# Two-block fp32 forward pass on one core: a rearranged state-space stage

## The chip, the cores and the metric

One NeuronCore of a Trainium2 chip runs the whole kernel as one program. The metric is the device time of one execution in microseconds (us). TensorE (PE) multiplies, VectorE (DVE) and ScalarE (ACT) work elementwise, GpSimd (POOL) does little here, SyncE (SP) only issues DMAs. Each engine runs its own instruction list in order; semaphores order the engines among each other. A DMA is issued from SyncE's or ScalarE's list (in the profile SPq, queue q1, and ACTq, queue q10) and moved by 16 DMA engines.

## The reference

512 tokens, model width 1024, everything in fp32. Two blocks follow each other; the change lies in the first one's first layer and in the modulation vectors.

```python
# first_block, per layer l (2 layers)
shift1, scale1, gate1, shift2, scale2, gate2 = split(silu(c) @ ada_w[l] + ada_b[l], 6)
h = rms_norm(x, norm1_g[l]) * (1 + scale1) + shift1
mix = s5_mixer(h, ...)          # layer 0; layer 1 is latent attention
x = x + gate1 * mix
h = rms_norm(x, norm2_g[l]) * (1 + scale2) + shift2
x = x + gate2 * ((silu(h @ w_gate) * (h @ w_up)) @ w_down)   # F = 2816

# s5_mixer: 64 groups of 16 channels, each a 64-dim complex diagonal state
bb = f * b                      # b: (64 groups, 64 states, 16 channels), complex
s_t = a * s_{t-1} + bb u_t;  y_t = Re(c s_t) + d_skip * u_t
g = gelu(y);  return g * sigmoid(g @ w_glu + b_glu)
```

The second block (gated linear attention, a convolution branch, another SwiGLU) takes six modulation vectors of its own, from `w_ada_2`; a key/value modulation comes from `kv_ada_w`.

## The kernel before

**Weights.** Large products (`phase_pe`, L526) split activations and weights into a high and a low part and run three matmuls per 128x128 tile. ScalarE makes the high part of a weight tile (`high_part`, L506), VectorE the low one (`low_part`, L512), SyncE loads the raw tile (`load_tile`, L375) once the one before it in its buffer is split. The phases run in a fixed order: glu, then gu0, dn0, gu1, dn1 (layer 0's SwiGLU in two halves), then attention and the rest.

**Modulation.** `silu(c) @ W` is cut into chunks of 2048 columns, each made of 8 slices (128 rows x 2048 columns, 1 MB). An early slice (`early_slice`, L409) is four fp32 products of one column of silu(c) with the slice, on TensorE, into the bank AD; the profile counts 8 matmuls for it. After 8 slices ScalarE evicts the bank (`ada_evict`, L472), TensorE turns it (`ada_turn`, L478), and VectorE adds the bias (`ada_take`, L487); slice 0 of the next chunk waits for that. There are 6 early chunks: the three of `ada_w[0]` and the three of `ada_w[1]`, slices 0 to 47. Slices 0 to 7 have a buffer each, from slice 8 on four buffers are shared (`load_early`, L402): slice s is loaded once slice s-4 is used. ScalarE issues slices 0 to 3, SyncE all others. Four late chunks follow in the glu and feed-forward phases with six buffers: the first and the last with slices on TensorE, the two between as weighted sums on VectorE (`late_sum_dve`, L450 and L452), closed by four products with ones (`late_sum_pe`, L460).

**State-space stage.** `start_*` and `params_*` load x, B, C and the parameters. x is turned on TensorE (L715), and all eight parts are copied out by ScalarE (L721). B is loaded with 64-byte runs into its final order, C is turned on TensorE (L915) behind a wait for both B and C, ScalarE copies it (L777), then squares the tokens for the norm (L786) and TensorE sums them (L803). VectorE multiplies B (L761 `Bb`), makes the first inputs block and the first powers block (`inputs_dve`, `powers_dve`, L761 `WB`, `CA`, L996, L997), and then takes the first modulation chunk and writes the normalized blocks (`normed_dve`, L895). The channels go through in eight steps k of 128 (`s5_pe`, `s5_dve`, `s5_act`). In step k, TensorE turns the block (L1206, L1215), makes the states' inputs (L1229), the outputs of step k-1 (`outputs_pe`, L1259 and L1263), the kernel of step k+1 (`kernel_pe`, L1243) and turns step k-1 back (`back_pe`, L1272), with four slices between, six in step 6 and ten from step 7 on. VectorE runs the scan (`scan_dve`, L1010 to L1024), norms block k+2, and makes inputs and powers of step k+2. ScalarE copies in between: step copy L1081, inputs L1091, blocks L1099, norm bias L901, eviction of the outputs (`back_act`, L1132), kernel copy L1107 with its store to DRAM L1111; `toeplitz_act` (L1122) loads the kernel back as a Toeplitz block that `outputs_pe` of the same k reads. Four blocks of sines (`angles_act`, L954 to L959) and the rope sines (`rope_trig_act`) are in steps 0 and 1. In step 6 TensorE waits first until VectorE has made the last powers.

**Tail.** ScalarE splits two glu tiles, evicts and gelus step 7, waits until all 48 slices are done (`wait_ge(S("early_done"), 48)`), writes the eight high parts of the stage's result (L1187), and evicts the last chunk; VectorE writes the low parts (L1064). TensorE turns the last chunk, then starts the glu phase, whose first tile takes the eight parts one by one.

## Time and profile before

| | |
|---|---|
| median of 3 runs | 2411.8 us (2411.66 to 2414.57) |
| the profiled execution | 2414.91 us, span 2413.1 us |
| mean granted TensorE clock | 0.966 of full |
| TensorE busy | 2249.8 us (93%) |
| VectorE, ScalarE busy | 1090.3 us (45%), 848.8 us (35%) |
| DMA | 269.97 MB, mean 112 GB/s |

Times of rows are us from the span's start, unless marked ns. The median is a time without profiling; a row belongs to the one profiled execution.

### The profile page before, as it was taken

To read this page: it belongs to the slowest core of one execution; us is meant where nothing else is said; L and a number is where in the kernel's file an instruction comes from. 1 tells how busy PE (TensorE), PEld (TensorE's weight loads), DVE (VectorE), ACT (ScalarE), POOL (GpSimd) and SP (SyncE) were. 2 spreads that over 40 slices of the span, in tenths; PEclk is the share of its full clock that TensorE was granted. 3 is DMA by queue.
4 is the path that set the end of the run, shared out by engine and by line. 5 is a ranking of instruction groups with operands and counts; after the bars stand their busy time and mean duration, and the time that the engine had idled before them with its cause. 6 is when DMAs were issued, how large, how long until landed. Compare 5 with 4: busy or idle time off the path is not lost.

```text
span 2413.1 us, 29168 instructions
## 1 busy us (share of the span) xinstructions
PE 2249.8 (93%) x11006; PEld 1728.1 (72%) x11006; DVE 1090.3 (45%) x1583; ACT 848.8 (35%) x1310; POOL 24.5 (1%) x29
## 2 busy tenths in 40 slices
PE   4687899999998789999999999999999998999997
PEld 2443668887866556888888777676888876888885
DVE  4783345444356664534324444555424334333332
ACT  4432332222245464423223344552222223322222
POOL 2100000000000000000000000000000000000000
PEclk8798999999999799999999999999999999999998
DMA  8477545545421003233233212222333322333331
GB/s 286 169 268 283 188 136 200 187 157 186 137 80 56 6 19 97 70 107 111 72 113 106 78 53 62 60 54 54 96 96 96 96 82 67 96 107 88 97 103 58
DMA packets 360891, 269.97 MB, mean 112 GB/s; under 512 B 20402, under 2 KB 346400, under 8 KB 350544
## 3 DMA queue, kind: packets, MB, share of 16 engines
q1 hardware_dynamic: 345548, 250.00, 33.6%
q10 hardware_dynamic: 15236, 18.50, 2.5%
q8 instruction: 72, 1.18, 0.2%
q14 instruction: 35, 0.29, 0.0%
HBM read 265.39 MB, written 3.08 MB: 111 GB/s over the span
## 4 chain that ended last, share of the span: by engine, by line
PE 82%; DVE 7%; ACT 3%; DVEq 2%; DMA 2%; issue 2%; ACTq 1%; SPq 0%; POOL 0%; POOLq 0%
PE G L526 59%; PE G L2072 9%; PE MS L1402 1%; PE AD L409 1%; DVE tb L606 1%; PE MS L2301 1%; DMA ada_s<-in_ada_w 1%; PE X L2282 1%; DMA TTall<-in_s_b_im 1%; PE X L2548 1%; DVE scan L761 1%; PE X L1814 1%; DVE wlo L512 1%; DVEq L605 1%; ACT whi L506 1%
## 5 line engine op out<-in xcount | busy, mean ns | idle before, releaser
L512 DVE TENSOR_TENSOR wlo<-raw,whi 128x1024 fp32r<-128x1024 f32 (+1 forms) x296 | 380.8, 1287 | 930.3 <-ACT whi L506 927.3
L506 ACT ACTIVATE whi<-raw 128x1024 fp32r<-128x1024 f32 (+1 forms) x296 | 328.1, 1109 | 904.8 <-PE G L526 757.4
L526 PE MATMUL G<-Ahi,whi 128*128 128x512 f32 x1440 | 573.3, 398 | 16.7 <-DVE Alo L611 9.3
L526 PE MATMUL G<-Ahi,wlo 128*128 128x512 f32 x1440 | 563.8, 392 | 0.0
L526 PE MATMUL G<-Alo,whi 128*128 128x512 f32 x1440 | 563.6, 391 | 0.0
L526 PEld LDWEIGHTS G<-Ahi,whi 128*128 128x128 f32 x1440 | 272.2, 189 | 89.4 <-issue 20.2
L526 PEld LDWEIGHTS G<-Ahi,wlo 128*128 128x128 f32 x1440 | 272.4, 189 | 58.6 <-issue 3.4
L526 PEld LDWEIGHTS G<-Alo,whi 128*128 128x128 f32 x1440 | 272.2, 189 | 57.4
L526 PE MATMUL G<-mhi,whi 128*128 128x512 f32 x528 | 211.8, 401 | 0.0
L526 PE MATMUL G<-mlo,whi 128*128 128x512 f32 x528 | 205.7, 390 | 0.0
L526 PE MATMUL G<-mhi,wlo 128*128 128x512 f32 x528 | 205.4, 389 | 0.0
L2072 PE MATMUL G<-Ahi,whi 128*128 128x512 f32 x320 | 131.8, 412 | 5.3 <-DVE Alo L611 3.8
L2072 PE MATMUL G<-Ahi,wlo 128*128 128x512 f32 x320 | 125.3, 391 | 0.0
L2072 PE MATMUL G<-Alo,whi 128*128 128x512 f32 x320 | 125.2, 391 | 0.0
L526 PEld LDWEIGHTS G<-mhi,whi 128*128 128x128 f32 x528 | 99.1, 188 | 25.1 <-issue 5.3
L526 PEld LDWEIGHTS G<-mhi,wlo 128*128 128x128 f32 x528 | 99.2, 188 | 23.2 <-issue 3.1
L526 PEld LDWEIGHTS G<-mlo,whi 128*128 128x128 f32 x528 | 99.1, 188 | 21.0
L1467 ACT ACTIVATE mhi<-tb 128x512 fp32r<-128x512 f32 (+1 forms) x66 | 41.7, 632 | 148.7 <-DVEq L1494 148.7
L2072 PEld LDWEIGHTS G<-Ahi,whi 128*128 128x128 f32 x320 | 60.3, 188 | 36.9 <-issue 20.0
L1408 ACT ACTIVATE sq<-xT 128x512 f32 (+1 forms) x48 | 30.3, 632 | 118.9 <-DVEq L1511 87.6
L2072 PEld LDWEIGHTS G<-Alo,whi 128*128 128x128 f32 x320 | 60.2, 188 | 13.2
L1498 DVE TENSOR_TENSOR mlo<-tb,mhi 128x512 fp32r<-128x512 f32 (+1 forms) x66 | 45.7, 693 | 52.3 <-ACT mhi L1467 52.3
(511 smaller groups left out, 2669.0 us busy)
## 6 DMA issues: line engine op xcount, KB each, us to landing
ada_s<-in_ada_w SPq DMA_DIRECT2D x40, 1024.0 KB, 8.0
raw<-in_w_in SPq DMA_DIRECT2D x64, 512.0 KB, 4.1
ada_ff<-in_w_ada SPq DMA_DIRECT2D x24, 1024.0 KB, 6.2
raw<-in_ffn_w_gate SPq DMA_DIRECT2D x44, 512.0 KB, 3.9
raw<-in_ffn_w_up SPq DMA_DIRECT2D x44, 512.0 KB, 3.9
raw<-in_ffn_w_down SPq DMA_DIRECT2D x32, 704.0 KB, 4.7
raw<-in_w_ffn_in SPq DMA_DIRECT2D x44, 512.0 KB, 3.8
raw<-in_w_ffn_out SPq DMA_DIRECT2D x16, 704.0 KB, 4.7
```

Source lines behind the costliest of these rows:

```text
L409: mm = E.eng.matmul(AD[32 * b:32 * b + n, :], cv, buf[:, b * 512:(b + 1) * 512], start=k == 0, stop=k == KD - 1)
L506: last = E.eng.activation(whi[j][:, k0:k0 + k, 0:c], raw[j][:, k0:k0 + k, 0:c], ACT.Copy)
L512: last = E.eng.tensor_tensor(wlo[j][:, k0:k0 + k, 0:c], raw[j][:, k0:k0 + k, 0:c], whi[j][:, k0:k0 + k, 0:c].bitcast(FP32), ALU.subtract)
L526: mm = E.eng.matmul(out_, a[j][:, k0 + kk, 0:c], b(kk), start=first and kk == 0 and n == 0, stop=last and kk == k - 1 and n == 2)
L605: E.eng.drain()
L606: E.eng.scalar_tensor_tensor(tb[k % 2][:, 0:n], src(k), a(k), rstd[:, 0:n], ALU.mult, ALU.mult)\
L761: E.eng.tensor_tensor(o, a, b, op)
L1402: E.eng.matmul(MS[:, :], ones, sq[j][:, :], start=first, stop=last).then_inc(S("sq_free"), 1)
L1408: E.eng.activation(sq[j][:, :], xT[:, bass.ds(n, 1), :].rearrange("p o t -> p (o t)"), ACT.Square)\
L1467: E.eng.activation(mhi[:, bass.ds(u, 1), :].rearrange("p o t -> p (o t)"), tb[1][:, :], ACT.Copy)\
L1498: E.eng.tensor_tensor(mlo[:, bass.ds(u, 1), :].rearrange("p o t -> p (o t)"), tb[1][:, :], mhi[:, bass.ds(u, 1), :].rearrange("p o t -> p ...
L2072: mm = E.eng.matmul(out_, a[j][:, kk, :], b[:, kk, :], start=first and n == 0, stop=last and n == 2)
```

## The change

1. **Chunks.** Chunk 2 of `ada_w[1]` (scale2 and gate2 of layer 1) leaves the early slices (40 instead of 48) and becomes a third VectorE sum among the late chunks (40 late loads instead of 32): dn0 now takes two sums per pair of tiles, gu1 one in eight pairs, and the last chunk's slices move from gu1 to dn1. In the loop each step has four slices.
2. **Start.** B is loaded as 32 rows of 8 KB and turned by 32 transposes into two PSUM banks, from which VectorE multiplies. The C transposes wait for C alone. ScalarE issues slices 0 to 7 and copies four x parts, VectorE the other four. ScalarE copies C after the token squares. All TensorE transposes of C and B come before slice 0; the norm sum before slice 2. VectorE makes the first powers after the two first normalized blocks.
3. **ScalarE in the loop.** In each step the output eviction and the kernel copy come before the norm bias; sines are spread over steps 0 to 2, rope sines and the gelu table go from step 1 to step 2; the Toeplitz load is issued after the blocks of its own step in each step, for step 7 too.
4. **Tail.** The last early chunk is evicted and turned before, high and low parts 0 to 6 are written before the eviction of step 7, part 7 after it.

```diff
+        Brow = [t[0:NPAIR, :, :].rearrange("p a b -> p (a b)")[:, 0:P * NCH] for t in (Wall, CAall)]
+        Braw = [X[1 + i].rearrange("p (c r) -> p r c", c=NCH) for i in range(2)]
...
+        ADA = ((A["ada_w"][0], 0, 1), (A["ada_w"][0], 1, 1), (A["ada_w"][0], 2, 1), (A["ada_w"][1], 0, 1),
+               (A["ada_w"][1], 1, 1), (A["kv_ada_w"], 0, 1), (A["w_ada_2"][0], 1, 1), (A["w_ada_2"][0], 2, 1),
+               (A["ada_w"][1], 2, 1), (A["w_ada_2"][0], 0, 2))
+        NEARLY_C = 5
+        NEARLY_S = NEARLY_C * KD
+        NADA = 5 * KD
...
-                d(Braw[i], A[f"s5_b_{w}"][0].rearrange("(r a) n p -> (a n) r p", a=2)).then_inc(S("dma_bc"), 16)
-            for s in range(4, 8):
-                load_early(E, s)
+                d(Brow[i], A[f"s5_b_{w}"][0].rearrange("(r a) n p -> r (a n p)", a=2)).then_inc(S("dma_b"), 16)
...
-            for n in range(4):
+            for n in range(KD):
                 load_early(E, n)
-            x_copy_act(E, 0, 4)
+            x_copy(E, 0, 4)
...
-            x_copy_act(E, 4, KD)
-            E.eng.wait_ge(S("ct_done"), E.nth("ct_done"))
+        def c_rows_act(E):
+
+            E.eng.wait_ge(S("turned_in"), 2)
...
+            c_rows_act(E)
             a.wait_ge(S("sq_free"), E.ahead("sq_free", 2))
             a.wait_ge(S("sd_free"), E.nth("sd_free"))
             a.activation(rstd[:, :], MS[:, :], ACT.Copy).then_inc(S("ms_done"), 1)
+            E.eng.wait_ge(S("xt_done"), KD)
...
+            x_copy(E, 4, KD)
...
             inputs_dve(E, 0)
-            E.eng.wait_ge(S("c_taken"), 1)
-            powers_dve(E, 0)
             ada_take(E, 0)
             gain_scale(E, acol[:, :], V_N1, mod[0][:, 8:16], 0)
             rms_dve(E)
             normed_dve(E, 0)
             normed_dve(E, 1)
+            E.eng.wait_ge(S("c_taken"), 1)
+            powers_dve(E, 0)
             inputs_dve(E, 1)
             powers_dve(E, 1)
...
+            E.eng.wait_ge(S("dma_c"), E.nth("dma_c", 2))
             E.eng.wait_ge(S("vec_ready"), 1)
             for i in range(2):
                 for t in range(8):
                     mm = E.eng.transpose(CBANK[2 * i + t // 4][0:NST, (t % 4) * P:(t % 4 + 1) * P], Craw[i][:, t, :],
                                          ident)
-            mm.then_inc(S("ct_done"), 1)
-            for s in range(2, 4):
+            mm.then_inc(S("turned_in"), 1)
+            E.eng.wait_ge(S("dma_b"), E.nth("dma_b", 2))
+            E.eng.wait_ge(S("xt_copied_2"), 4)
+            for i in range(2):
+                rows = Brow[i].rearrange("r (m c) -> r c m", c=NCH)
+                for c in range(NCH):
+                    mm = E.eng.transpose(X[1 + i][:, c * NPAIR:(c + 1) * NPAIR], rows[:, c, :], ident[0:NPAIR, 0:NPAIR])
+            mm.then_inc(S("turned_in"), 1)
+            E.eng.wait_ge(S("silu_c"), 1)
+            for s in range(2):
                 early_slice(E, s)
             token_rms_pe(E)
-            for s in range(4, 8):
+            for s in range(2, KD):
                 early_slice(E, s)
             ada_turn(E, 0)
             E.eng.wait_ge(S("c_taken"), 1)
             turn_inputs_pe(E, 0)
             E.eng.wait_ge(S("ms_done"), E.ahead("ms_done", 1))
-            kernel_pe(E, 0)
...
+            def low(k):
                 E.eng.wait_ge(S("hi_ready"), E.nth("hi_ready"))
                 v.tensor_tensor(Alo[:, k, :], hS[:, k, :], Ahi[:, k, :].bitcast(FP32), ALU.subtract)\
                     .then_inc(S("part_ready"), 1)
+
+            for k in range(KD - 1):
+                low(k)
+            out_dve(E, 7)
+            v.drain().then_inc(S("s5_out"), 1)
+            low(KD - 1)
             v.drain().then_inc(S("in_ready"), 1)
-            ada_take(E, 5)
+            ada_take(E, 4)
...
                     blocks_act(E, 0)
-                    toeplitz_act(E, 0)
+                    kernel_act(E, 0)
                 else:
                     steps_act(E, k)
                 if k < 7:
                     turn_steps_act(E, k + 1)
                     inputs_act(E, k + 1)
-                else:
-                    ada_evict(E, 4)
                 if k > 0:
                     blocks_act(E, k)
-                    if k < 7:
-                        toeplitz_act(E, k)
-                if k < 6:
-                    normed_act(E, k + 2)
+                toeplitz_act(E, k)
                 if k == 6:
                     kernel_act(E, 7)
                 if k > 0:
                     back_act(E, k - 1)
                 if k < 6:
                     kernel_act(E, k + 1)
-                if k > 1:
+                if k < 3:
+                    angles_act(E, k + 1)
+                if k == 2:
+                    rope_trig_act(E)
+                    preset(E, ACT.Gelu_apprx_tanh)
+                if k < 6:
+                    normed_act(E, k + 2)
+                if k == 3:
+                    gelu_act(E, 0)
+                if k > 2:
                     gelu_act(E, k - 2)
                 if k in (1, 3, 5):
                     ada_evict(E, k // 2 + 1)
-                if k == 0:
-                    angles_act(E, 1)
-                if k == 1:
-                    angles_act(E, 2)
-                    angles_act(E, 3)
-                    rope_trig_act(E)
-                    preset(E, ACT.Gelu_apprx_tanh)
-                if k == 6:
-                    toeplitz_act(E, 7)
             high_part(E, "glu", 0, 0)
             high_part(E, "glu", 1, 1)
             gelu_act(E, 6)
+            E.eng.wait_ge(S("early_done"), NEARLY_S)
+            ada_evict(E, 4)
+            a.drain()
+
+            def high(k):
+                a.activation(Ahi[:, k, :], hS[:, k, :], ACT.Copy).then_inc(S("hi_ready"), 1)
+
+            for k in range(KD - 1):
+                high(k)
             back_act(E, 7)
             gelu_act(E, 7)
             a.drain()
-            E.eng.wait_ge(S("early_done"), 48)
-            for k in range(KD):
-                a.activation(Ahi[:, k, :], hS[:, k, :], ACT.Copy).then_inc(S("hi_ready"), 1)
-            ada_evict(E, 5)
+            high(KD - 1)
...
+                    kernel_pe(E, 0)
...
+                slices(s, 11 + 4 * k)
+                if k < 6:
+                    kernel_pe(E, k + 1)
+                if k > 0:
+                    back_pe(E, k - 1)
+                slices(11 + 4 * k, 12 + 4 * k)
             outputs_pe(E, 7)
-            slices(42, 45)
+            ada_turn(E, 4)
             back_pe(E, 7)
-            slices(45, 48)
-            ada_turn(E, 5)
...
+            first, n = {"gu0": (6, 1), "dn0": (17, 2), "gu1": (25, 1), "dn1": (36, 1)}.get(ph, (None, 0))
             if first is None:
                 return None
-            return {i: lambda s=first + i: load_late(E, s) for i in range(TILES[ph] // 2)}
+
+            def loads(i):
+                for s in range(first + n * i, first + n * i + n):
+                    load_late(E, s)
+            return {i: lambda i=i: loads(i) for i in range(TILES[ph] // 2)}
...
+                return {0: lambda: late_sum_pe(E, 6), 1: lambda: ada_turn(E, 6)}
             if ph == "gu1":
-                return {6: lambda: late_sum_pe(E, 8), 7: lambda: ada_turn(E, 8),
-                        8: lambda: late_slice(E, 24), 9: lambda: late_slice(E, 25)}
+                return {0: lambda: late_sum_pe(E, 7), 1: lambda: ada_turn(E, 7),
+                        8: lambda: late_sum_pe(E, 8), 9: lambda: ada_turn(E, 8)}
+            if ph == "dn1":
+                return {0: lambda: late_slice(E, 32), 1: lambda: late_slice(E, 33)}
...
+                sums = {"gu0": {i: (5 + i,) for i in range(3, 11)},
+                        "dn0": {i: (16 + 2 * i, 17 + 2 * i) for i in range(4)},
+                        "gu1": {i: (24 + i,) for i in range(8)}}[ph]
+                takes = {"gu0": {3: 5}, "dn0": {1: 6}, "gu1": {1: 7, 9: 8}}[ph]
```

## Rows read from the trace of the kernel before

**Rows 1.** The page's part 4: chain that ended last, share by engine.

```profile
PE 82%; DVE 7%; ACT 3%; DVEq 2%; DMA 2%; issue 2%; ACTq 1%; SPq 0%; POOL 0%; POOLq 0%
```

**Rows 2.** Windows: length, PE PEld DVE ACT POOL busy, clock, DMA share, GB/s.

```profile
202.00:246.00 44.00, 30.94 (x292) 11.66 (x281) 11.02 (x23) 9.29 (x15) 0.00 (x0) 0.84 1.01 352
...
320.00:600.00 280.00, 279.81 (x1250) 227.55 (x1250) 127.73 (x114) 77.38 (x93) 0.00 (x0) 1.00 0.54 180
```

**Rows 3.** Timeline of the start: start, us, line, operation, [idle before, releaser].

```profile
12.61 15.93 SPq L663 DMA_DIRECT2D TTall<-in_s_b_im  x1
...
33.49 1.84 PE L915 MATMUL X<-con,TTall 128*64 128x128 f32 x8 [2.35 <-DMA TTall<-in_s_b_im]
...
41.62 1.06 ACT L786 ACTIVATE CA<-turned 128x1024 f32<-128x1024 f32 x1
...
50.84 3.49 PE L409 MATMUL AD<-ada_first,cact 128*1 128x512 f32 x16
...
54.16 1.89 PE L409 MATMUL AD<-hS,cact 128*1 128x512 f32 x16
...
58.19 1.78 DVE L895 SCALAR_TENSOR_TENSOR tb<-xT,acol,rstd 128x512 f32<-128x512 f32 x1 [0.26 <-issue]
```

**Rows 4.** DMA: queues in 18 to 20 us; one issue with us to landing.

```profile
q10 hardware_dynamic: 112, 0.79, 95.9%
q1 hardware_dynamic: 112, 0.03, 6.7%
...
TTall<-in_s_c_im SPq DMA_DIRECT2D x1, 256.0 KB, 21.7
```

**Rows 5.** Timeline: eight transposes of 64 rows at half clock.

```profile
110.98 1.12 PE L1215 MATMUL X<-con,Hn 64*128 64x64 f32 x8 [5.13 <-ACTq L1083]
```

**Rows 6.** Windows around the C transposes (columns as in rows 2).

```profile
34.00:36.00 2.00, 2.00 (x12) 1.59 (x11) 1.97 (x4) 0.00 (x0) 0.00 (x0) 0.50 0.98 410
...
38.00:40.00 2.00, 0.87 (x11) 0.00 (x0) 1.93 (x5) 1.94 (x6) 0.00 (x0) 1.00 0.98 414
```

**Rows 7.** Timeline: the last operation of the first powers block.

```profile
44.95 0.75 DVE L997 SCALAR_TENSOR_TENSOR CA<-CA,c 128x576 f32<-128x576 f32 x1
```

**Rows 8.** Timeline of steps 1 to 3, ScalarE and VectorE.

```profile
105.18 0.63 ACT L954 ACTIVATE turned<-ang 128x512 f32<-128x512 f32 x1
...
109.85 1.05 ACT L1081 ACTIVATE Hn<-X 64x512 f32<-64x512 f32 x2
...
116.01 1.42 DVE L761 TENSOR_TENSOR scan<-X,turned 128x256 f32<-128x256 f32 x4 [9.55 <-PE X L1229]
...
129.62 1.07 ACT L1081 ACTIVATE Hn<-X 64x512 f32<-64x512 f32 x2 [0.23 <-PE X L1206]
...
135.00 1.42 DVE L761 TENSOR_TENSOR scan<-X,turned 128x256 f32<-128x256 f32 x4 [1.84 <-PE X L1229]
```

**Rows 9.** Timeline of step 6's end, step 7 and the tail.

```profile
204.16 0.71 PE L1272 MATMUL X<-con,Ypk 64*128 64x64 f32 x8
...
211.95 1.89 PE L409 MATMUL AD<-ada_s,cact 128*1 128x512 f32 x8 [7.09 <-DMA ada_s<-in_ada_w]
...
216.05 1.92 PE L1206 MATMUL X<-con,tb 128*64 128x128 f32 x8
...
232.45 0.44 PE L1263 MATMUL G<-TTall,Ust 128*64 128x128 f32 x4
...
234.95 1.20 ACT L1132 ACTIVATE Ypk<-G 64x512 f32<-64x512 f32 x2
...
245.24 4.27 ACT L1187 ACTIVATE Ahi<-hS 128x512 fp32r<-128x512 f32 x8 [6.30 <-PE AD L409]
...
250.95 0.77 PE L526 MATMUL G<-Ahi,whi 128*128 128x512 f32 x1
```

**Rows 10.** Late sums by tile, ns min/median/max; window of a dn0 pair.

```profile
L452 DVE SCALAR_TENSOR_TENSOR ada_sum<-ada_ff,cact,ada_sum x14: 2341/2346/2348, 378.4 to 559.7; 128x2048 f32<-128x2048 f32 x14
...
469.00:484.00 15.00, 15.00 (x70) 12.41 (x69) 5.94 (x6) 2.76 (x2) 0.00 (x0) 1.00 0.66 228
```

More of the change, by code:

```diff
@@ L160, in program @@
         c2 = sb("c2", [P, 4, RB + 1, NCH], where=s5a)
-        Wst = [[sb(f"Wst{k}{i}", [P, 4, P], where=s5a) for i in range(2)] for k in range(2)]
+        Wall = sb("Wall", [P, 4, 4 * P], where=s5a)
+        Wst = [[Wall[:, 2 * k + i, :].rearrange("p (a b) -> p a b", a=4) for i in range(2)] for k in range(2)]
         ada_first = [sb(f"ada_first{i}", [P, 2 * D], where=s5a) for i in range(2)]
@@ L209, in program @@
         xn = turned[:, :, :]
-        CA = [[sb(f"CA{k}{i}", [P, 4, RB + 1, NCH], where=s5) for i in range(2)] for k in range(2)]
+        CAall = sb("CAall", [P, 4, 4 * (RB + 1) * NCH], where=s5)
+        CA = [[CAall[:, 2 * k + i, :].rearrange("p (a b c) -> p a b c", a=4, c=NCH) for i in range(2)] for k in range(2)]
         CA2 = sb("CA2", [P, 2, 4 * (RB + 1) * NCH], where=s5)
@@ L1184, in s5_act @@
             a.drain()
-            E.eng.wait_ge(S("early_done"), 48)
-            for k in range(KD):
-                a.activation(Ahi[:, k, :], hS[:, k, :], ACT.Copy).then_inc(S("hi_ready"), 1)
-            ada_evict(E, 5)
+            high(KD - 1)
         def turn_inputs_pe(E, k):
@@ L1332, in early_sp @@
                 load_tile(E, "glu", n, n)
-            for s in range(44, 48):
-                load_early(E, s)
         def phase_sp(E, ph, hooks=None):
@@ L1581, in ffn_hooks_act @@
         def ffn_hooks_act(E, ph):
-            if ph in ("gu0", "dn0", "gu1"):
-                i, c = {"gu0": (2, 6), "dn0": (0, 7), "gu1": (6, 8)}[ph]
-                return {i: lambda: ada_evict(E, c)}
+            rows = {"gu0": {2: 5}, "dn0": {0: 6}, "gu1": {0: 7, 8: 8}, "dn1": {}}.get(ph)
+            if rows is not None:
+                return {i: lambda c=c: ada_evict(E, c) for i, c in rows.items()} or {99: None}
             if ph == "gu2":
@@ L3047, in _ @@
             turn_steps_act(E, 0)
-            kernel_act(E, 0)
             normed_act(E, 1)
```

120 lines of the change are left out of this document (47 added, 73 removed).

## The prediction, made before the changed kernel was run

> **What bounds the kernel now.** I read the chain that ended last first: TensorE holds 82% of it, almost all in the 3-pass weight products at L526 [rows 1]. The stage table then says where TensorE is not the bound. From 320 to 600 us it is busy 279.81 of 280.00 us, so there a microsecond of VectorE or DMA work is free and one of TensorE is not. From 202 to 246 us it is busy 30.94 of 44.00 us at a clock of 0.84 while the DMA engines stand at a share of 1.01 [rows 2]. The change edits the first 251 us, so I went on with the timeline of that stretch: the start, the eight steps of the state-space loop, the tail. Every term below is a wait of that timeline that goes, moves or appears.
>
> **Start, up to the first normalized block (58.19 us).** SyncE's issue of the second B load alone takes 15.93 us; TensorE (for the C transposes behind the same semaphore) and VectorE wait for its landing until 33.49. ScalarE waits for the turned C, copies it, and only then starts the token squares at 41.62. Modulation slices 4 to 7 are queued behind the norm on TensorE and start at 50.84, though slices need nothing of it; the last ends at 56.05 [rows 3].
>
> After the change the squares start when ScalarE has finished the trigonometry (it has nothing to wait for there), VectorE takes four of its x copies, and C is copied after the squares. TensorE becomes the long chain: C transposes, B transposes, slices 0 and 1, the norm sum, slices 2 to 7. When does C land? Its second half is issued after some 6 us of small loads and lands 21.7 us later, near 28. In 18 to 20 us both queues moved exactly 112 packets each, though 0.79 MB against 0.03 MB [rows 4]: one packet of C's 256 bytes for one of 8 KB of the modulation weights. The Trainium skill, DMA: Bandwidth & Descriptors, Queues, rings and completion order, states such a round robin by packets, and the trace agrees. So twice as many modulation slices on ScalarE's queue can only delay C, and B stands behind C. B however is now 64 packets of 8 KB instead of 8192 of 64 bytes: 4 to an engine. I take C at 28.5 and B at 31.5. C's first eight transposes took 1.84 us at half clock [rows 3], 16 take 3.6: done at 32. B's 32 transposes have no row; the nearest are eight of 64x64 in 1.12 us at half clock [rows 5] (0.14 each, 4.5 us) and C's (0.23 each, 7 us); I take the small ones, as B's have 32 columns: done at 36.5. Two slices cost 1.89 us at full clock and 3.49 at half [rows 3]. Eight at full: 7.6. The norm sum, eight small products, I estimate at the 1.84 of C's eight: 2. Then eviction, turn and take as before (56.05 to 58.19): 2.1. Sum 48.2; I take 49, bounds 46 (C not delayed, small transposes) and 55.
>
> The other bound is the clock. The Trainium skill, TensorE: Matmul & The Clock Gate, Part 4: PE-mode transpose, says that transposes do not raise the clock; by it all eight slices would run at half clock, 14 us instead of 7.6, and the block would come at 55. The trace says otherwise: granted clock 0.50 in 34 to 36 us, where TensorE ran only transposes, and 1.00 in 38 to 40 us [rows 6]. I keep the full clock.
>
> Against it stands the order on VectorE. The first powers block (six operations of 0.75 us, started some 0.7 apart: 4.3 us) used to fill the wait for the slices (it was done at 45.70) [rows 7] and now lies between the first normalized block and the first scan. VectorE was already back to back there, so it costs its full 4.3. **Start: 9.2 - 4.3 = +4.9 us** (bounds -1 and +8).
>
> **Loop, steps 0 to 5.** Step 0 is VectorE's own work, unchanged. In step 1 ScalarE no longer stands at the norm wait before it evicts, and one of two angle blocks, the rope sines and the Gelu table go to step 2. VectorE waited 9.55 us for scan 2; without it the powers of step 3 are just finished when the states come: **+9.5**. What left step 1 is from 105.18 to 109.85, 4.7 us, plus the shift of 0.7; in step 2 they now stand between the kernel copy and the step copy at 129.62, where ScalarE had only 0.23 us idle. That copy begins the chain that VectorE waits 1.84 us for at 135.00, so all of it shows: **-4.6** [rows 8]. In steps 3 and 5 VectorE alone is the bound (before scan 4 and after scan 5 it has no wait in the trace), and in step 4 the slices wait for the modulation taken after the scan, as before: **0**.
>
> **Step 6.** Six slices before the next turn, with four buffers: after the back-turn at 204.16 TensorE waits 7.09 us for slice 36 and turns the next block at 216.05. With a chunk fewer only slice 35 is left there, already moved in exchange from before the back-turn. From 204.87 to 216.05 are 11.2 us. Slice 36 now stands before the states of step 7, some 6 us after the back-turn, at 211; it landed at 211.95, its load starting as early after as before: **+11**, bounds +8 and +11.
>
> **Step 7 and tail.** Outputs of step 7 end at 232.89. Then came: eviction at 234.95, the wait for slice 47 until 245.24 (6.30 us on ScalarE), eight high parts in 4.27 us, the last modulation turn, first product at 250.95: 18.1 us after the outputs [rows 9]. After: two weight splits, gelu 0.6, eviction 0.6, seven high parts 3.7 (all startable before the outputs end), then eviction 1.2, back-turn 0.7 and the first product, because parts 0 to 6 are ready; 21 products cover the last part's 3 us. The weight tiles land some 3 us before the outputs end, so about 4 us of the high parts stick out: first product 6.3 us after the outputs. The last Toeplitz load is issued in step 7 instead of step 6 and has 9 us before its use; it moves 0.5 MB beside four slices. I allow 2 us for it and slices 37 to 39. **+10**, bounds +6 and +12.
>
> **Later.** The chunk comes back as eight VectorE sums in dn0 and gu1 at 2.35 us, hidden: a dn pair has VectorE busy 5.94 of 15.00 us with one sum in it. The eight more loads are hidden too: that pair moved 228 GB/s at a share of 0.66 [rows 10]. On TensorE, which is the bound there, four ones-products (as long as one slice) and four turns are new: 0.95 + 0.7 = **-1.7**. The same eight two-row slices move from gu1 to dn1.
>
> Sum: 4.9 + 9.5 - 4.6 + 11 + 10 - 1.7 = 29.1 us of the profiled execution's 2414.91. That one lies 3.1 us above the median 2411.8; I take the difference off the median: 2382.7, so **2383 us**.
>
> **Rivals.**
> *The start gives nothing.* If eight large loads starve C and B, or the transposes are slow, the first block comes at 55 and the 4.3 us of powers eat the rest: gain 23, 2389 us. For: the one-to-one packets. Against: C needed only until 28.1 with the same arbitration. 0.14.
> *Step 2 is absorbed.* If the sines find a gap in ScalarE's 9 us wait before the scan, the -4.6 goes: 2378; with the start at its best, 2375. Against: program order puts them after the kernel copy. 0.12.
> *The last loads stick.* Slice 36 holds the states of step 7, or the Toeplitz block comes 4 us late behind 8 KB packets: gain 22, 2390 us. For: slice 36 landed 7.09 us after TensorE stood ready for it, with the DMA engines full [rows 2, 9]. 0.14.
> *Nothing moves.* If the 44 us were bound by TensorE after all; its 30.94 busy us speak against. 2412, 0.02.
> *Slower.* One place: the dn0 and gu1 pairs. Their VectorE orders two sums of 2.35 us (dn0), one (gu1), ahead of the next low split. If the split comes after the tile before it ends, TensorE waits in each of 12 pairs. The place turns the result only when each wait exceeds 29/12 = 2.4 us, a whole sum: 2.35 on 8 more sums is 19 us, 2402 us; with waits of 3 us 2419 us. Against: 5.94 + 2.35 of 15.00. 0.04.
>
> **Chances.** The sum as worked out 0.54. About 0.2% (5 us) is what a measurement of this kernel can tell from none. Faster 0.94, same 0.02, slower 0.04. The range goes from the best start with step 2 absorbed (2373) to two of the losing rivals together (2397).
>
> **What the profile of after would show.** First normalized block near 49 us and scan 0 about 5 us earlier; VectorE without a wait before scan 2; the step copy of step 3 later after the kernel copy than 0.9 us, with sines between; no wait over 3 us for a slice at the end of step 6; first product near 220 us; sums of 128x2048 at 24, not 16, and TensorE still busy throughout 320 to 600. Wrong would be: C landing past 32 us; TensorE waiting for the Toeplitz load; TensorE waits for low splits in dn0.

## The result, and the profile after

The changed kernel takes 2390.74 us (median of 4 runs, 2387.76 to 2391.8), the kernel before 2411.97 (4 runs): ratio 0.991, 95% interval 0.9894 to 0.9926, so 21.2 us less. I had said 2383, 29.1 less. The profiled execution took 2387.76 against 2414.91, which is 27.2 less; it is 3 us under its median, and the profiled execution of before is 3 us above its own, so some 6 us of that difference are not the change's.

The chain of waits is as before [rows 1]: the weight products keep it. The first line is the page's share by engine, the others are windows (columns as in rows 2). The stage from 320 to 600 us is still TensorE's, and the one after the last scan now stands at 208 to 216:

```profile
PE 82%; DVE 7%; ACT 3%; DVEq 3%; DMA 2%; issue 2%; ACTq 1%; SPq 0%; POOL 0%; POOLq 0%
...
320.00:600.00 280.00, 280.00 (x1255) 227.97 (x1255) 145.11 (x122) 77.42 (x92) 0.00 (x0) 1.00 0.58 198
...
188.00:192.00 4.00, 4.00 (x40) 2.70 (x38) 3.72 (x10) 0.59 (x1) 0.00 (x0) 0.54 0.34 95
192.00:196.00 4.00, 4.00 (x49) 2.15 (x53) 1.69 (x6) 0.73 (x2) 0.00 (x0) 1.00 0.10 21
...
204.00:208.00 4.00, 4.00 (x64) 2.73 (x59) 3.32 (x8) 0.00 (x0) 0.00 (x0) 1.00 1.00 408
208.00:212.00 4.00, 3.00 (x32) 1.00 (x34) 3.08 (x8) 1.82 (x3) 0.00 (x0) 1.00 1.09 185
212.00:216.00 4.00, 1.27 (x14) 0.54 (x8) 0.00 (x0) 0.00 (x0) 0.00 (x0) 0.95 0.96 171
```

DMA is nearly idle at 188 to 196 (shares 0.34 and 0.10) and full at 208 to 216, there at 171 to 185 GB/s where almost nothing but slices ran at 408 just before. This contrast decides the tail, below.

The start, as a timeline (start, us, line, operation, idle before). It answers to rows 3 and 7:

```profile
28.73 1.91 PE L928 MATMUL X<-con,TTall 128*64 128x128 f32 x8 [5.32 <-DMA TTall<-in_s_c_im]
...
32.85 1.98 PE L936 MATMUL X<-con,Wall 32*128 32x32 f32 x16 [0.51 <-DMA CAall<-in_s_b_im]
34.65 1.95 PE L936 MATMUL X<-con,CAall 32*128 32x32 f32 x16
36.53 3.59 PE L417 MATMUL AD<-ada_s,cact 128*1 128x512 f32 x16
40.05 1.84 PE L818 MATMUL MS<-sq,con 128*128 128x128 f32 x8
...
49.28 2.51 DVE L911 SCALAR_TENSOR_TENSOR tb<-xT,acol,rstd 128x512 f32<-128x512 f32 x2 [0.26 <-issue]
```

The reader sees the chain that I had added up: C at 28.5 (28.73), B's transposes done at 36.5 (36.6), the normalized block at 49 (49.28). Steps 1 and 2 answer to rows 8:

```profile
103.91 1.42 DVE L773 TENSOR_TENSOR scan<-X,turned 128x256 f32<-128x256 f32 x4 [1.87 <-PE X L1253]
...
114.93 0.59 ACT L1130 ACTIVATE KT<-MS 48x512 f32<-48x512 f32 x1 [4.87 <-PE MS L1267]
...
116.39 0.63 ACT L974 ACTIVATE turned<-ang 128x512 f32<-128x512 f32 x1 [0.87 <-ACT KT L1130]
...
121.67 1.05 ACT L1104 ACTIVATE Hn<-X 64x512 f32<-64x512 f32 x2
...
127.45 1.42 DVE L773 TENSOR_TENSOR scan<-X,turned 128x256 f32<-128x256 f32 x4 [6.38 <-PE X L1253]
```

The sines stand between the kernel copy and the step copy, as foreseen, and VectorE waits 6.38 us for scan 3; but there is a hole of 4.87 us ahead of the kernel copy. The tail answers to rows 9:

```profile
203.19 0.60 ACTq L1145 DMA_DIRECT2D TTall<-blocks  x1
...
204.49 1.42 DVE L773 TENSOR_TENSOR scan<-X,turned 128x256 f32<-128x256 f32 x4 [4.79 <-PE X L1253]
...
211.72 1.04 PE L417 MATMUL AD<-ada_s,cact 128*1 128x512 f32 x8 [1.00 <-DMA ada_s<-in_ada_w]
...
215.49 1.07 PE L1283 MATMUL G<-CAall,Sst 64*64 64x128 f32 x8 [2.73 <-DMA TTall<-blocks]
...
218.22 1.06 ACT L515 ACTIVATE whi<-raw 128x1024 fp32r<-128x1024 f32 x1 [0.56 <-DMA raw<-in_s_w_glu]
...
220.50 3.75 ACT L1205 ACTIVATE Ahi<-hS 128x512 fp32r<-128x512 f32 x7
...
224.15 1.18 ACT L1155 ACTIVATE Ypk<-G 64x512 f32<-64x512 f32 x2
...
226.18 0.79 PE L535 MATMUL G<-Ahi,whi 128*128 128x512 f32 x1
```

Two transfers are late here: the last Toeplitz block holds the output products until 215.49, and the second glu weight tile lands at 218.22, 17.7 us after its issue, with seven copies and the last Y copy queued behind it on ScalarE.

One edit that "The change" does not name bears on this. The kernel before issued the first two glu weight tiles ahead of its last four slices (44 to 47); the changed kernel issues them behind its last slice. SyncE's lists, first before, then after (the x4 of the last line takes in the next two tiles, issued from 219 us on):

```profile
220.67 4.73 SPq L375 DMA_DIRECT2D raw<-in_s_w_glu  x2
227.63 7.48 SPq L402 DMA_DIRECT2D ada_s<-in_ada_w  x4
```

```profile
196.24 3.65 SPq L410 DMA_DIRECT2D ada_s<-in_ada_w  x4
199.93 21.00 SPq L378 DMA_DIRECT2D raw<-in_s_w_glu  x4
```

**Scan by scan.** Each step is the time from one scan's start to the next (first operation of the scan on VectorE). "Tail" goes from the last scan to the first glu product, "rest" from there to the end of the span. Step k goes from scan k to scan k+1. All are profiled executions; the last three columns are experiments below.

| | before | after | chunk alone (e9) | e6 | e8 |
|---|---|---|---|---|---|
| scan 0 at | 69.55 | 64.91 | 68.23 | 69.09 | 64.40 |
| step 0 | 20.52 | 20.75 | 20.51 | 20.99 | 20.36 |
| step 1 | 25.94 | 18.25 | 25.92 | 18.12 | 16.32 |
| step 2 | 18.99 | 23.54 | 18.98 | 23.58 | 19.63 |
| steps 3 to 5 | 59.24 | 60.14 | 60.33 | 59.53 | 59.91 |
| step 6 | 28.58 | 16.90 | 18.22 | 15.72 | 15.73 |
| tail | 28.13 | 21.69 | 24.36 | 14.40 | 14.40 |
| rest | 2162.2 | 2159.7 | 2159.2 | 2158.7 | 2158.0 |

### The profile page after: what moved, and what is told of

The parts are those of the page before. It is cut to its first block, busy times and chain, and to the rows that moved or that the text cites. A ratio compares the mean times of both kernels' runs of the same rounds, so it can differ in the third digit from the quotient of the medians.

```text
span 2385.9 us, 29083 instructions
## 1 busy us (share of the span) xinstructions
PE 2240.0 (94%) x10982; PEld 1728.6 (72%) x10982; DVE 1110.4 (47%) x1595; ACT 846.0 (35%) x1306; POOL 24.4 (1%) x29
## 3 DMA queue, kind: packets, MB, share of 16 engines
q1 hardware_dynamic: 336844, 245.80, 33.5%
## 4 chain that ended last, share of the span: by engine, by line
PE 82%; DVE 7%; ACT 3%; DVEq 3%; DMA 2%; issue 2%; ACTq 1%; SPq 0%; POOL 0%; POOLq 0%
PE G L535 60%; PE G L2089 9%; PE MS L1412 1%; DVE tb L615 1%; PE AD L417 1%; PE MS L2318 1%; PE X L2299 1%; DMA CAall<-in_s_b_im 1%; DMA raw<-in_s_w_glu 1%; PE X L2565 1%; PE X L1831 1%; DVE wlo L521 1%; DVEq L614 1%; ACT whi L515 1%; DVEq L774 1%
## 5 line engine op out<-in xcount | busy, mean ns | idle before, releaser
L1418 ACT ACTIVATE sq<-xT 128x512 f32<-128x512 f32 (+1 forms) x48 | 30.3, 632 | 117.7 <-DVEq L1521 86.6
L2089 PEld LDWEIGHTS G<-Alo,whi 128*128 128x128 f32 x320 | 60.5, 189 | 13.2
```

What stands on the lines that cost most here:

```text
L1418: E.eng.activation(sq[j][:, :], xT[:, bass.ds(n, 1), :].rearrange("p o t -> p (o t)"), ACT.Square)\
L2089: mm = E.eng.matmul(out_, a[j][:, kk, :], b[:, kk, :], start=first and n == 0, stop=last and n == 2)
```

## The experiments

Medians are compared with the changed kernel's 2390.74 and, for the parts made alone, with the runs of the kernel before that were measured beside them. A "ratio" or "of before" is always against those runs of before, with its 95% interval.

### e1 to e3: is the tail held by the Toeplitz block or by the weight tiles?

e1 issues the last Toeplitz load at the end of step 6:

```
-                toeplitz_act(E, k)
+                if k < 7:
+                    toeplitz_act(E, k)
...
+                if k == 6:
+                    toeplitz_act(E, 7)
```

> The changed kernel with one edit: the load of the last Toeplitz block is issued at the end of step 6 again, as before the change, not in step 7. In the changed kernel it is issued at 203.2 us and holds up the last output products until 215.5, and the first glu product comes at 226.2. Theory A (the two glu weight tiles, which land at 216.6 and 218.2, and the split, the eviction and the seven copies that ScalarE runs behind them, set the first product): the block lands by 211, the last output products start near 212.8, but ScalarE still comes to the last Y copy near 224, the first product stays within 1 us of 226.2 and the time within 1.5 us of 2390.7. Theory B (the late Toeplitz block sets it): the first product comes 3 to 4 us earlier, 2387.

e2 places the weight splits behind the copies and the last Y copy (low_part likewise behind out_dve):

```
-            high_part(E, "glu", 0, 0)
-            high_part(E, "glu", 1, 1)
             gelu_act(E, 6)
...
             back_act(E, 7)
+            high_part(E, "glu", 0, 0)
+            high_part(E, "glu", 1, 1)
             gelu_act(E, 7)
```

> The changed kernel with one edit: on ScalarE and VectorE the seven copies and differences of A, the last Y copy and the last output sum are placed ahead of the splits of the first two glu weight tiles. The last Toeplitz block still lands at 215.5. Theory A (the weight tiles gate the first product by ScalarE's order): the copies run near 213.5 to 217.3, the last Y copy at 221 (end of the output products), the split behind it, and the first product comes near 223.2, 3 us earlier; 2387.7. Theory B (the Toeplitz block and what follows its products alone set it): the Y copy was not held, the first product stays near 226, 2390.7, or later by the 2.1 us of the splits that now stand behind the Y copy, 2393.

e3 has both edits.

> Both edits together, on the changed kernel: the Toeplitz load back at the end of step 6, and the weight splits behind the copies and the last Y copy. Theory A with the Toeplitz block as the second gate behind it: output products from 212.8 to 216.5, Y copy at 217.3, first product at 219.5 to 220.5, 6 to 6.5 us earlier; 2384.5. If one of the two alone were the gate, this kernel would give no more than that one alone (3 to 4 us). If the DMA engines are simply full until 218, so that the blocks only change places, the weight tiles land later than 218.2 and the gain is below 3.

Measured: 2393.66 (e1), 2392.83 (e2), 2394.11 us (e3); tails 22.65, 21.35 and 22.04 us. None of them gained anything. In e1 the output products no longer wait for the Toeplitz block, but the last but one and the last slice came later:

```profile
215.15 1.88 PE L417 MATMUL AD<-ada_s,cact 128*1 128x512 f32 x8 [3.01 <-DMA ada_s<-in_ada_w]
...
218.01 1.89 PE L417 MATMUL AD<-ada_s,cact 128*1 128x512 f32 x8
219.83 1.12 PE L1286 MATMUL G<-CAall,Sst 64*64 64x128 f32 x8
```

Its last scan began at 206.53, so the outputs start 13.3 us behind it, against 11.0 in the changed kernel. In e2 the copies of A were done by 220.8, but the Y copy waited for the output products until 225.31 and the splits came behind it. So the Toeplitz block alone is not the gate: the time is the one that theory A of e1 gives, but the block's early load delayed slices, and the outputs did not start at 212.8. ScalarE's order alone is not the gate either (theory B in e2), and neither are the two together. What holds is the last sentence of e3's expectation: the DMA engines are full, and blocks only change places.

### e6: give the tail's DMA work an idle time

```
-            for s in range(KD, NEARLY_S):
+            for s in range(KD, 36):
                 load_early(E, s)
             for n in range(2):
                 load_tile(E, "glu", n, n)
+            for s in range(36, NEARLY_S):
+                load_early(E, s)
```

> The changed kernel with one edit: SyncE issues the loads of the first two glu weight tiles ahead of slice 36, not behind slice 39. Between 180 and 196 us the DMA engines are nearly idle (0.16 and 0.36 of their time), while slices 36 to 39 wait for their buffers; from 200 to 216 they are full. Theory A (what the tail lacks is DMA time between 200 and 218: swapping ScalarE's order or issuing the Toeplitz block earlier only moved the wait, the first product came 21.7, 22.7, 21.4 and 22.0 us after the last scan began): the tiles land before 195, the last slice and the Toeplitz block within 13 us after the last scan began... worked from the changed kernel: slice 39 and the block by 210 to 211, the last output products 211.7 to 215.4, seven copies 213 to 217, Y copy 217, first product near 219.5 instead of 226.2, counted from the last scan 15 us instead of 21.7; total 6 to 7 us less than the changed kernel. Theory B (ScalarE's and TensorE's own chain behind the last scan is 21 us long whatever lands when): no change within 1 us.

Measured 2382.94 us (4 runs, ratio to before 0.9886, interval 0.9868 to 0.9905), 7.8 less than the changed kernel. The tiles are now issued at 177.19, ahead of the last four slices, which is the place that they had in the kernel before. The tail is 14.40 us, 7.3 less (e8, with the same edit, has 14.40 too), and windows of the same stretch read:

```profile
184.00:188.00 4.00, 4.00 (x20) 3.51 (x18) 0.06 (x1) 2.20 (x3) 0.00 (x0) 0.50 0.86 216
...
212.00:216.00 4.00, 2.83 (x32) 1.12 (x24) 3.64 (x6) 3.80 (x7) 0.00 (x0) 1.00 0.26 73
```

Timeline of the same kernel, whose last scan began at 207.03:

```profile
177.19 3.79 SPq L378 DMA_DIRECT2D raw<-in_s_w_glu  x2
...
215.48 0.65 PE L1283 MATMUL G<-CAall,Sst 64*64 64x128 f32 x8 [1.13 <-DMA TTall<-blocks]
...
221.43 0.50 PE L535 MATMUL G<-Ahi,whi 128*128 128x512 f32 x1
```

Theory A is shown by size and place, to within 1 us of what was expected: the two tiles, loaded in the full stretch, were the price, and the change had put them there itself.

### e4 and e10: the start

e4 builds the first powers block ahead of the take again:

```
             inputs_dve(E, 0)
+            E.eng.wait_ge(S("c_taken"), 1)
+            powers_dve(E, 0)
             ada_take(E, 0)
...
-            E.eng.wait_ge(S("c_taken"), 1)
-            powers_dve(E, 0)
```

> The changed kernel with one edit: VectorE builds the first block of powers again ahead of the take of the first modulation row. VectorE is idle there from 44.5 to 48.5 us, and the block of powers takes 4.3 us (51.7 to 56.0) behind the normalized blocks. Theory A (my term of the start: the move costs what it adds ahead of the first scan): the first normalized block stays at 49.3 to 49.8, the first scan comes at 60.9 instead of 64.9, and all later scans with it: 4 us, 2386.7. Theory B (the first two steps are set by ScalarE and TensorE, so that a first scan that is earlier is given back by the third): the scan of step 2 moves by under 1 us and the time stays at 2390.7 within 1 us.

Measured 2398.05 us (2397.48 to 2400.94), 7.3 more. Scan 0 came at 64.61 with C landed at 31.08, but step 1 grew from 18.25 to 23.33. The first states and the first kernel product came later (63.99, against 59.90), so did the first Toeplitz load (71.44, against 66.66), and TensorE met it missing:

```profile
71.44 0.70 ACTq L1145 DMA_DIRECT2D TTall<-blocks  x1
...
87.23 1.12 PE L1283 MATMUL G<-CAall,Sst 64*64 64x128 f32 x8 [2.86 <-DMA TTall<-blocks]
```

Both theories missed, the first with the wrong sign. The move that I priced at -4.3 us is worth more than it costs. Counted from C's landing, this kernel's scan 0 is some 2 us earlier (33.5 us behind it, against 35.4 on average in the seven profiles listed below), its first glu product 2.1 us later (199.5 us behind it, against 197.4 in the changed kernel). Of the remaining 5 us I know only that they lie behind the first product (rest 2165.4 in the one profile).

e10 is the kernel before with the changed start alone (the diff of the start functions, and kernel_act and kernel_pe of block 0 moved into step 0).

> The kernel before with the start of the change alone (B as rows turned on TensorE, half of the turned x copied by VectorE, all eight first slices issued by ScalarE, normalized blocks ahead of the powers of block 0, first kernel product behind the first states). Theory A (what the runs so far say): the first scan comes at 65 to 69 instead of 69.6, with C's landing as the cause of the spread; 1 to 2 us less than before, 2410.5. Theory B (my term of the start, 4.9 us): 2407. If the new place of the first kernel product delays the first Toeplitz block where ScalarE's order is the old one, step 0 or 1 is longer and the time is 2412 or more.

Measured 2413.78 us (11 runs, 2406.86 to 2424.21) against 2411.96 (17 runs, 2408.99 to 2415.39): ratio 1.0001, interval 0.9989 to 1.0014. The start alone gives nothing that can be measured, at most 2.7 us, and widens the spread from 6 to 17 us. In its one profile C landed at 32.80 and scan 0 began at 68.30, 1.25 us earlier than in the first profile of before; steps 0 to 4 are as before, but steps 5 and 6 and the tail are longer by 0.73, 1.55 and 0.45 us, so that its first glu product is 1.4 us later (252.36). With 48 early slices TensorE waits for slices there (2.48 and 5.91 us at the end of step 6), whatever the start gained. So e10 prices the start in the old loop, not in the changed one.

### e12 and e5: why the start gives so little

> The kernel before once more, for its profile alone: is its start as variable as that of the changed one, and how long is what follows the first glu product? If C's landing varies here too, the first scan is not at 69.6 but anywhere in 67 to 73. If only the changed start varies, it is at 69.6 within 0.5. From the first product to the end of the span the changed kernel and its variants took 2158 to 2165 us with the same code, the kernel before 2162.2; it should fall into this band.

2410.55 us. TensorE's first C transposes, in this order: in e12 ([rows 3] has the other profile of before), in e9, which has the old start, and in e3, the latest of the profiles with the changed start:

```profile
33.52 1.92 PE L915 MATMUL X<-con,TTall 128*64 128x128 f32 x8 [2.80 <-DMA TTall<-in_s_b_im]
```

```profile
33.55 1.16 PE L921 MATMUL X<-con,TTall 128*64 128x128 f32 x8 [1.95 <-DMA TTall<-in_s_b_im]
```

```profile
34.53 1.91 PE L928 MATMUL X<-con,TTall 128*64 128x128 f32 x8 [11.11 <-DMA TTall<-in_s_c_im]
```

With the old start C and B had both landed by 33.49, 33.52 and 33.55. With the changed one, C alone had landed at 28.73, 31.31, 31.97, 33.09, 33.19, 33.29 and 34.53 (after, e11, e1, e2, e7, e6, e3), and scan 0 began at 64.91, 66.43, 67.42, 68.34, 68.60, 69.09 and 69.33: mean 67.7. Before it began at 69.55, 68.78 and 68.23 (e9): mean 68.9. The start gives 1.1 us on average, and my profile of the changed kernel is its luckiest start. (Two more profiles have the same start loads: C at 31.08 in e4 and at 32.80 in e10.)

The landing of C by itself says why. Here are the loads of its second half, with us from issue to landing, in the second profile of before, in the changed kernel and in e3:

```profile
TTall<-in_s_c_im SPq DMA_DIRECT2D x1, 256.0 KB, 21.8
...
TTall<-in_s_c_im SPq DMA_DIRECT2D x1, 256.0 KB, 22.3
...
TTall<-in_s_c_im SPq DMA_DIRECT2D x1, 256.0 KB, 28.1
```

With the old start it took 21.7 ([rows 4]), 21.8 and 21.4 us, with the changed one 22.3 to 28.1. The changed start no longer makes C wait for B, which had come last, and at the same time it made C land later, by up to 6.7 us.

e5 gives slices 4 to 7 back to SyncE, behind B:

```
-            for n in range(KD):
+            for n in range(4):
                 load_early(E, n)
...
+            for s in range(4, KD):
+                load_early(E, s)
```

> The changed kernel with one edit: the first slices 4 to 7 (4 MB) are issued by SyncE behind the loads of B, as before the change, not by ScalarE ahead of them. In four kernels with the changed start the imaginary part of C landed at 28.7, 32.0, 33.1 and 34.5 us, and the first scan followed 36.2, 35.5, 35.3 and 34.8 us behind it (64.9 to 69.3). Theory A (the eight slices on ScalarE's queue share the DMA engines with C's and B's small runs and set when they land, and how much by chance): C lands by 27 and with less spread, the slices 4 to 7 land last, near 42 to 44, so that the last of their products end near 46 and the first scan comes at 62 to 65; 2387 to 2389. Theory B (C's descriptors are what is slow, whoever shares the engines): C lands at 28 to 35 as before, the first scan at 65 to 69, and the time is that of the changed kernel, 2390.7 to 2393, or more if the slices are late.

2387.4 us (5 runs, 0.9897 of before, interval 0.988 to 0.9913); C at 30.39, scan 0 at 65.14; in e8, which has the same edit, 29.57 and 64.40. Two landings, both earlier than six of the seven above, and 3.3 us off the median: it leans to theory A, but the intervals overlap with the changed kernel's and C never landed by 27. Likely, not shown. And it would not be the whole: with four slices on ScalarE's queue, as before the change, C still took 24.0 and 23.2 us, 1.4 to 2.6 more than with the old start. The other difference beside it is B's form, rows of 8 KB in place of 64-byte runs on C's own queue; no run changes that alone.

### e7 and e11: step 1 and step 2

e7 moves the sines into ScalarE's hole ahead of the kernel copy, in steps 0 to 2:

```
-                if k < 6:
-                    kernel_act(E, k + 1)
                 if k < 3:
                     angles_act(E, k + 1)
                 if k == 2:
                     rope_trig_act(E)
                     preset(E, ACT.Gelu_apprx_tanh)
+                if k < 6:
+                    kernel_act(E, k + 1)
```

> The changed kernel with one edit: in steps 0 to 2 ScalarE computes the angles' sines (in step 2 also the rotary sines and the switch to the Gelu table) ahead of the kernel copy, where in step 2 it is idle for 4.9 us (from 110.1 to 114.9), and not behind it. Theory A (my term of step 2: the 4.6 us that step 2 lost are this block of 4.6 us ahead of the normalized block and the step copy): step 2, from scan 2 to scan 3, falls from 23.5 us to 19 to 20; step 1 may gain up to 1; total 4 us less than the changed kernel. Theory B (the step copy of step 3 waits for something else, so the block is hidden): step 2 stays at 23.5 within 1 us and the time with it.

2388.16 us (4 runs, 2387.62 to 2389.07), 2.6 less. Step 1 is 16.32 us, step 2 20.63, together 4.8 less; step 4 took 1.65 more. Theory A, with a little less in step 2 and more in step 1. A timeline line of step 2 shows the kernel copy of this kernel with the sines done before it and still 2.67 us idle:

```profile
118.23 0.59 ACT L1130 ACTIVATE KT<-MS 48x512 f32<-48x512 f32 x1 [2.67 <-PE MS L1267]
```

e11 undoes "evictions ahead of the norm wait": normed_act stands again directly behind toeplitz_act.

> The changed kernel with one part undone: ScalarE's normalized block of each step stands again behind the Toeplitz load and ahead of the copies of Y and of the kernel, so that these wait for VectorE's normalized block. Theory A (my term of step 1, measured as 8.0 us, is this order): step 1 rises from 18.3 us to 24 to 26, steps 2 to 5 by up to 1 each; 8 to 10 us more than the changed kernel, 2400. Theory B (step 1's gain came from the sines of angles 3, the rotary sines and the table switch, 4.6 us that moved from step 1 to step 2): step 1 rises by 3 or less, 2394.

2389.99 us (6 runs; 0.9914 of before, interval 0.99 to 0.9929), the time of the changed kernel; step 1 is 19.02 us, 0.8 more, which is no more than the spread: e3 and e5, without this edit, have 18.98 and 19.01. ScalarE waits 11.64 us for VectorE's normalized block again, and it doesn't matter:

```profile
93.88 0.72 ACT L917 ACTIVATE hS<-tb,mod 128x512 f32<-128x512 f32 x1 [11.64 <-DVE tb L911]
...
100.08 0.60 ACT L481 ACTIVATE arow<-AD 128x512 f32<-128x512 f32 x1
100.58 1.06 ACT L1104 ACTIVATE Hn<-X 64x512 f32<-64x512 f32 x2
```

From the normalized block to the step copy ScalarE needed 12.81 us before (97.04 to 109.85) and needs 6.70 here: the 4.7 us of sines and table are gone, and the eviction at L481, ahead of which ScalarE stood idle for 2.32 us before, now has the other sines in front of it. Here is the kernel before at that place:

```profile
97.04 0.72 ACT L901 ACTIVATE hS<-tb,mod 128x512 f32<-128x512 f32 x1 [11.69 <-DVE tb L895]
...
101.92 0.60 ACT L472 ACTIVATE arow<-AD 128x512 f32<-128x512 f32 x1 [2.32 <-PE AD L409]
```

### e9: the chunk alone

The kernel before with 40 early slices, the new late tables and hooks, and the old start and orders.

> The kernel before with one part of the change alone: the sixth modulation chunk is computed in the later phases (40 early slices, not 48; the late tables and hooks as in the changed kernel); start, ScalarE's order in the steps and the order of the tail stay as before. Theory A (the terms of step 6 and of the tail are the chunk's): scans 0 to 6 as before (69.6 to 194.2, within the start's spread), step 6 falls from 28.6 to 17 us, step 7 and tail from 28.1 to 22 to 24, later phases 2 us later; 15 to 16 us less than before, 2396. Theory B (the new orders carry the tail, so that without them the products of A and the weight tiles give it back): 9 to 11 us less, 2402.

2398.72 us (5 runs, 2395.91 to 2400.57), ratio 0.9945, interval 0.9932 to 0.9957: 13.2 less than before, between the theories. It has the glu tiles behind the last slice, as the changed kernel has. Step 6 gives 10.4 and the tail 3.8 (table). With the rest of the change the tail is 2.7 shorter still (24.36 to 21.69): here ScalarE's eight copies still stand behind the last Y copy, and TensorE's last wait is for the modulation eviction behind them:

```profile
235.78 1.12 PE L484 MATMUL AD<-con,arow 128*128 128x128 f32 x4 [6.46 <-ACT arow L478]
```

### e8: the three edits that helped

e5, e6 and e7 together, on the changed kernel.

> The changed kernel with the edits of the three kernels before: slices 4 to 7 behind B, glu tiles ahead of slice 36, sines ahead of the kernel copy. Theory A of each, added: start 2 to 4, step 2 4, tail 6 to 7: 12 to 15 us less than the changed kernel, 2377 to 2380. If they are not independent (a step that starts earlier waits longer for slices or for the Toeplitz blocks), 6 to 9 us less, 2383.

2371.87 us (5 runs, 2370.49 to 2375.34; 0.9835 of before, interval 0.9821 to 0.9849): 40.3 us less than the kernel before, 18.9 less than the changed one, above the 12 to 15 I expected and above the sum of the three medians (3.3 + 7.8 + 2.6 = 13.7). First glu product at 210.75, 15.4 us ahead of the changed kernel's profile; its start is early too (64.40), which is some 3 us against the mean start of 67.7, and makes 18 or so. This version beats both kernels.

## Why the prediction held, and where it was off

The time lay in my range and on the side that I gave 0.94, 7.7 us above my value. The signs and places of the terms are right but for the powers; the start and the tail each fell some 4 us short and step 1 another 2; the total stayed in the range (2373 to 2397) because the range was wide enough for both. Two of the three signs that I had named as "wrong would be" came true: C landed past 32 us in most profiles with the changed start (not in the changed kernel's own), and TensorE waited 2.73 us for the last Toeplitz load. Two of my rivals came true by about half, "the start gives nothing" (priced at -6 us, measured -3.8) and "the last loads stick" (-7, measured -3.6 in the tail, by the Toeplitz block and not by slice 36). The terms, against the table; the start is taken from the means over profiles, because single profiles mislead there:

| term | predicted | measured |
|---|---|---|
| start | +4.9 | +1.1 (e10, in the old loop: 0, up to 2.7) |
| step 0 | 0 | -0.2 |
| step 1 | +9.5 | +7.7 |
| step 2 | -4.6 | -4.6 |
| steps 3 to 5 | 0 | -0.9 |
| step 6 | +11 | +11.7 |
| step 7 and tail | +10 | +6.4 |
| later | -1.7 | not seen: rest 2158.6 to 2162.2 before, 2158.0 to 2165.4 with it |
| sum | 29.1 | 21.2 (medians: 21.2) |

That the sum meets the medians this closely is partly chance: only the start is a mean, the other rows are one pair of profiles, and the rest of the span is not in it. Other profiles with the same code in a row give step 1 from 18.1 to 19.0, step 6 from 15.7 to 16.9 and the tail from 21.6 to 22.1 us.

**Start.** The failed step is "I take C at 28.5". When C came at 28.73 the links behind it came as added up (B at 32.8 for 31.5, but TensorE was busy with C until 32.3; B's transposes done at 36.6 for 36.5; the block at 49.28 for 49). But C came there once in seven. I had written that eight slices on ScalarE's queue can only delay C and that C past 32 us would prove me wrong; it landed past 32 in four of seven (five of nine with e4 and e10). My first rival, "the start gives nothing", had the block at 55; in the seven profiles it came at 49.28 to 53.65. Its mechanism, that large loads starve C, fits the landings, but only leans on e5. Between 18 and 20 us the two queues again moved packets nearly one for one, ScalarE's 8 KB ones against C's 256 bytes:

```profile
q10 hardware_dynamic: 112, 0.79, 96.0%
q1 hardware_dynamic: 113, 0.03, 6.7%
```

The -4.3 of the powers failed in sign (e4): on VectorE's own list it does cost its time, but the first normalized block is also the head of the chain to the first Toeplitz block, which step 1 needs.

The clock term was off as well. I kept the full clock for all eight slices, but in every profile with the changed start the first two took 3.20 to 3.59 us, at or near half clock; the other six went at 1.90 a pair. That is up to 1.7 us of the chain. In the changed kernel the granted clock stayed at 0.50 through all transposes (28.73 to 36.6) and up to 40 us. In e2 it did rise while TensorE ran nothing but transposes (33.09 to 40.77), and fell again to 0.56 in 40 to 42; the line is a window, columns as in rows 2:

```profile
38.00:40.00 2.00, 2.00 (x21) 2.00 (x20) 0.00 (x0) 1.79 (x5) 0.00 (x0) 1.00 1.02 406
```

So both happen with this code, and my row of 38 to 40 us could not promise either.

**Step 1.** The size was nearly right, the first of its two reasons wrong. I named that ScalarE no longer stands at the norm wait and that sines and table leave the step. e11 puts the wait back, and it costs 0.8 us at most. What carried the step, by e11's rows, is that 4.7 us of sines and table left it and that the 2.3 us idle ahead of the modulation eviction was filled; no run puts the sines back, so this is read, not tested. The missing 1.8 us are the angle block that stayed: with it ahead of the kernel copy step 1 is 16.32 us (e7), VectorE's own work without a wait, 9.6 less than before.

**Step 2.** Right in place and size. But "all of it shows" was a matter of position only: the hole ahead of the kernel copy takes most of it (e7). The rival "absorbed" was one swap away.

**Step 6.** Right: slice 36 no longer stands there. Of the 11.7, 10.4 come with the chunk alone (e9).

**Tail.** The failed step is "I allow 2 us for it and slices 37 to 39". What follows the output products shrank from 18.1 us to 5.3 (I had 6.3). But the outputs themselves end 16.4 us after the last scan instead of 10.1: 6.3 us, not 2, for one Toeplitz block, two weight tiles and the slices, all issued between 196 and 204 us. I looked at the block's size and its nine us, not at the sum of what was on the DMA engines in that time, and not at the glu tiles, which the change moved behind the last slice; with them back ahead of the last four slices the tail is 14.40 us (e6), 13.7 less than before, where I had forecast 10. "The weight tiles land some 3 us before the outputs end" was true (218.22 and 220.84), but only because both were late.

**Later.** The sums are 24 (21 and 3 of the first kind), TensorE is busy 280.00 of 280.00 us from 320 to 600, so they are hidden. Whether the 1.7 us on TensorE are there can't be told: the rest of the same code varies by 7 us between profiles. The mean granted clock of the whole execution varies too (0.967 to 0.977), but it does not order them: e11 had 0.977 and a rest of 2160.4 us, e5 0.971 and 2158.1.

## What to carry to other kernels

When a wait for a transfer goes, look at the DMA row of the windows around it before moving issues within it: if it is full there and empty ahead, try a load with free buffers in the empty stretch (7.8 us here); swapping the loads or the order of their readers gave nothing in three kernels. When loads are taken off a queue's list, look where that leaves the others on it: here two tiles slid behind the last slice unpriced. A profile is one draw: scan the same stage in several profiles before a term is booked to it; here the start's 4.6 us of the first pair of profiles were 1.1 on average. And a block taken off one engine's list is not free or dear by itself: ask which chain its neighbour heads (e4), and whether the engine has a hole one place further up (e7).

## What the runs showed of the hardware

- How long a 256 KB load of 256-byte runs takes to land beside a second full queue is not stable: 22.3 to 28.1 us from issue with the changed start, 5.8 us between profiles, but 21.4 to 21.8 in three profiles of the old start. B's loads behind it, in rows of 8 KB, were there up to 4 us later. When C and B both had small runs and ScalarE's queue held four slices, both had landed at the same time to 0.06 us in those three profiles.
- With the DMA engines at a full share, weight tiles in 512-byte runs moved fewer bytes than slices in 8 KB packets, and not always the same number: mixed with the Toeplitz block 171 to 185 GB/s (208 to 216 us, changed kernel), nearly alone 305 GB/s (184 to 186 us, e6), against 408 to 424 for slices. No run tells what sets the 171 apart from the 305.
- Packets were not always shared one for one. From 209 to 216 us ScalarE's queue (the Toeplitz block) moved 99 packets while SyncE's moved 1606. The Trainium skill, DMA: Bandwidth & Descriptors, Queues, rings and completion order, gives a round robin by packets between queues that have work; at 18 to 20 us the rows agree with it, here they do not. No run here tells why, and no row shows whether both queues had work on every engine all the time:

```profile
q1 hardware_dynamic: 1606, 0.82, 73.2%
q10 hardware_dynamic: 99, 0.37, 26.4%
```
